# A four-layer network on one core: the low half of each weight slab, subtracted by POOL instead of DVE in the stages that convolve

## The reference

```python
x = x + ssd_mixer(rmsnorm(x));   x = x + conv_ffn(rmsnorm(x))          # 528 tokens
x = x + stick_breaking_attention(...);  x = x + conv_ffn(rmsnorm(x))   # 528
x = x + chunked_rel_attention(rmsnorm(x)); x = x + relu2_mlp(rmsnorm(x))  # 512
x = x + gated_deltanet(rmsnorm(x));        x = x + relu2_mlp(rmsnorm(x))  # 512

def conv_ffn(u):      # depthwise causal convolution, 3 taps, behind the up projection
    g, val = split(causal_dwconv(u @ w_up, conv_w, conv_b)); return (silu(g) * val) @ w_down
# ssd_mixer:      silu(causal_dwconv(u @ w_in[xbc])), 4 taps, then a scan; z is not convolved
# gated_deltanet: silu(causal_conv(h @ w_in[qkv])),   4 taps, then a scan; z is not convolved
```

## Time and profile before

| | |
|---|---|
| median of the runs | 3454.03 us |
| the profiled execution's own time | 3458.24 us |
| its span, first to last instruction | 3456.5 us |
| TensorE (PE) busy | 3210.4 us, 93% of the span |
| VectorE (DVE) busy | 1955.8 us, 57% |
| ScalarE (ACT) busy | 1015.3 us, 29% |
| GpSimd (POOL) busy | 412.0 us, 12% |
| `w_low` subtraction on DVE | 426 instructions, 551.9 us, 1297 ns each |

### The profile page before, as it was taken

The page is one execution under the profiler, slowest core; times in us unless marked ns, Lnnn a source line. Parts: engine busy times, 40 slices in busy tenths (PEclk is TensorE's granted clock), DMA queues, the critical chain, the costliest instruction groups (busy, mean ns, idle before and its releaser), DMA issues.

```text
span 3456.5 us, 49739 instructions
## 1 busy us (share of the span) xinstructions
PE 3210.4 (93%) x19456; PEld 2758.6 (80%) x19456; DVE 1955.8 (57%) x2939; ACT 1015.3 (29%) x1634; POOL 412.0 (12%) x446
## 2 busy tenths in 40 slices
PE   6997879999999999989996999999998988899998
PEld 6995559999998777889995667788876677778886
DVE  5746874647573333574666555544466666664444
ACT  3233332322232434331222333222232522232221
POOL 2000222000020111300005001100010122220002
PEclk9998989999999999999998999999999999999999
DMA  3220002222221000122222222222222200022222
GB/s 115 85 85 31 1 13 91 80 80 85 92 92 62 25 25 31 57 78 90 87 86 73 74 74 68 85 97 91 97 85 79 67 1 1 1 73 97 91 97 79
DMA packets 64344, 235.14 MB, mean 68 GB/s; under 512 B 7248, under 2 KB 7248, under 8 KB 63952
## 3 DMA queue, kind: packets, MB, share of 16 engines
q1 hardware_dynamic: 62928, 229.05, 19.9%
q0 software_dynamic: 1280, 4.20, 0.4%
HBM read 231.12 MB, written 2.10 MB: 67 GB/s over the span
## 4 chain that ended last, share of the span: by engine, by line
PE 58%; DVE 14%; issue 6%; ACT 5%; POOL 2%; DVEq 1%; ACTq 0%; POOLq 0%
PE ps L268 35%; PE ps L297 8%; DVE conv_acc L322 5%; ACT w_high L230 3%; PE ps L1031 2%; PE ps L1024 2%; DVE conv_acc L319 1%; PE ps L1046 1%; PE ps L1014 1%; PE ps L1331 1%; PE ps L1678 1%; PE ps L1359 1%; POOL sqa L377 1%; PE ps L1673 1%; DVE t L436 1%
## 5 line engine op out<-in xcount | busy, mean ns | idle before, releaser
L268 PE MATMUL ps<-x_hi,w_high 128*128 128x264 f32 (+1 forms) x2968 | 764.2, 318 | 71.1 <-DVE w_low L235 33.2
L268 PE MATMUL ps<-x_lo,w_high 128*128 128x264 f32 (+1 forms) x2968 | 755.9, 315 | 0.0
L268 PE MATMUL ps<-x_hi,w_low 128*128 128x264 f32 (+1 forms) x2968 | 754.9, 315 | 0.0
L235 DVE TENSOR_TENSOR w_low<-w_raw,w_high 128x1024 fp32r<-128x1024 f32 x426 | 551.9, 1297 | 262.0 <-ACT w_high L230 261.1
L268 PEld LDWEIGHTS ps<-x_hi,w_high 128*128 128x128 f32 x2968 | 489.8, 189 | 126.9 <-issue 57.7
L230 ACT ACTIVATE w_high<-w_raw 128x1024 fp32r<-128x1024 f32 x426 | 446.0, 1050 | 435.0 <-DMA w_raw<-in_slabs 423.7
L268 PEld LDWEIGHTS ps<-x_lo,w_high 128*128 128x128 f32 x2968 | 487.8, 189 | 34.5 <-issue 1.9
L268 PEld LDWEIGHTS ps<-x_hi,w_low 128*128 128x128 f32 x2968 | 488.8, 190 | 33.3
L268 PE MATMUL ps<-mid_hi,w_high 128*128 128x264 f32 (+1 forms) x1280 | 374.3, 338 | 22.1 <-DVE mid_lo L421 20.5
L268 PE MATMUL ps<-mid_lo,w_high 128*128 128x264 f32 (+1 forms) x1280 | 374.6, 338 | 0.0
L268 PE MATMUL ps<-mid_hi,w_low 128*128 128x264 f32 (+1 forms) x1280 | 373.6, 337 | 0.0
(11 more groups left out here) (339 smaller groups left out, 4323.3 us busy)
## 6 DMA issues: line engine op xcount, KB each, us to landing
w_raw<-in_slabs SPq DMA_DIRECT2D x426, 512.0 KB, 3.3
rel_bias<-in_rel POOLq DMA_DIRECT2D x16, 256.0 KB, 2.9
h<-in_x SPq DMA_DIRECT2D x1, 2112.0 KB, 8.6
out_y<-h SPq DMA_DIRECT2D x8, 256.0 KB, 2.1
consts<-in_consts SPq DMA_DIRECT2D x1, 1032.0 KB, 13.1
par<-in_params SPq DMA_DIRECT2D x1, 346.5 KB, 9.0
```

Of the source, the lines that this page charges most:

```text
L235: dve.tensor_tensor(w_low[:, n % RING, :], w_raw[:, n % RING, :], w_high[:, n % RING, :].bitcast(F32), ALU.subtract).then_inc(S("w_lo"), 1)
L268: mm = pe.matmul(ps[:, 2 * tslot + k, 0:n], w, a[:, kb, c:c + n], start=first, stop=fin)
```

## The change

In the 136 steps of the convolving stages the subtraction leaves DVE's queue and goes into POOL's. `lows_pool` is the same loop of four slabs on POOL: wait for `w_hi`, subtract, count up `w_lo`. Since two engines now count up one counter, the engine that takes over first waits until the other has done its share (`lows_begin`). In `dn_v` POOL's loop is written out, so that five squares of the l2 norm stand between the subtractions. Nothing else changes on ACT, TensorE or SP.

```diff
+        def lows_begin(eng, name):
+            eng.wait_ge(S("w_lo"), SLAB0[name] + AHEAD)
+        def lows_pool(pool, name):
+            lows_begin(pool, name)
+            steps(pool, name, lambda j, i: slab_lo(pool, SLAB0[name] + j, i))
...
                     take_scaled(dve, name, j, i, pad[:, j % 2, 3:3 + LA], LA)
-                    slab_lo(dve, SLAB0[name] + j, i)
                     conv_taps(dve, name, j, i, 3, lambda t: rcol("ffn_conv_w", tile * 3 + t, 12 * i), conv0, LA)
...
                 pair += k
+                lows_begin(dve, f"ffn{layer}_down{r}")
                 residual_dve(dve, f"ffn{layer}_down{r}", LA, split if r == 2 else None)
...
                 take_scaled(dve, name, j, i, pad[:, j % 2, 3:3 + T], T)
-                slab_lo(dve, SLAB0[name] + j, i)
                 dve.wait_ge(S("conv_used"), first + j + 1 + 4 * i)
...
+            lows_begin(dve, "z")
             scaled_stage_dve(dve, "z", lambda k: tile_of(z_t, k, LA), LA)
...
         def ssd_pool(pool):
             stats_pool(pool, 0, LA)
+            lows_pool(pool, "bc")
+            lows_pool(pool, "xs")
...
+            lows_begin(dve, "dn_z")
...
         def dn_pool(pool):
-
+            lows_pool(pool, "dn_qk")
+            lows_begin(pool, "dn_v")
+            for j in range(2):
+                slab_lo(pool, SLAB0["dn_v"] + j)
...
                     .then_inc(S("l2_sq"), 1)
+                if t < 5:
+                    for j in (2 + t,) if t < 4 else (6, 7):
+                        slab_lo(pool, SLAB0["dn_v"] + j)
...
             def pool(e):
+                for r in range(len(FFN_ROUNDS)):
+                    lows_pool(e, f"ffn{layer}_up{r}")
                 stats_pool(e, n_next, LA)
```

## The result

The changed kernel takes 3446.72 us (median of 12 runs, 3433.23 to 3449.17) beside 3459.0 us for the kernel before (12 runs, 3450.45 to 3466.95): ratio 0.9963, 95% interval 0.995 to 0.9975. It is faster by 0.37%, inside the range of 3419 to 3465 but above the forecast's own 3420 to 3443, on the side that was held likeliest, and by about half of what was forecast: 12.3 us between the medians where the sum said 24.

What follows compares the result with a forecast made beforehand. PE is busy 93%; convolving stages lie above its pace, `xs` by a ring through DVE and ACT. Terms -9.6 - 11 - 4 + 0.2 = -24 us took the profiled 3458.2 to 3434, median 3430; range 3419 to 3465.

Steps and rivals of the forecast that it cites:

- the ring through ACT: Convolving stages: DVE's taps wait for ACT's copy, 6.32 us a slab in `xs` against PE's 5.87; the change cuts this.
- POOL and DVE exclude each other: When both read two things in SBUF, each waits for the other's whole instruction, less overlaps of 0.14 and 0.19 us.
- The term D: Length of one POOL subtraction of 1024 columns: taken as 2.3 us, lowest 2.07, highest 2.6; delays DVE by D - 0.47.
- The prediction's own table: Whole kernel's time by length of POOL's subtraction: 2.07 gives about 3421 us, 2.4 gives 3440, 2.5 3453, 2.6 3466.
- `up1`, `up2`: nothing, but without slack: Both feed-forward layers, 56 slabs: four DVE steps take 23.2 us against PE's 23.5, so no gain or loss.
- one of them hides under the wait or a take: `up1`, `up2`: of four subtractions one is hidden by 0.7 to 0.9 us, bringing four DVE steps from 24.0 to 23.2.
- the path from the last tile to `mid_lo`: `down1`, `down2`: exchanges 1.23 and 0.50 us of waiting for 1.83, with DVE behind by part of a step: +1.3 each.
- `dn_qk` 96 us: Deltanet: DVE bounds, 16 steps of 5.75 us plus some 4 us for the start give 96 us, -9.
- `dn_z` and `dn_out` untouched: Deltanet stages without the moved subtraction: forecast to change by 0.
- Rival 2: Slower: feed-forward stages lose their cover from a POOL subtraction of 2.42 us on; at 2.6, +12 us, 3466; chance 0.14.
- rival 3: POOL gets its turn only when DVE is idle; +1 us or more on 136 slabs, beyond 3550 us; chance 0.02.
- rival 4: The change does less than it says, because POOL is held by what stands ahead in its queue; no chance given.

Runs made afterwards that it cites:

- e4_up0: The changed kernel, but in `up1` and `up2` of both feed-forward layers DVE subtracts again; 3433.21 us, ratio 0.9937 to the kernel before.
- e3_ffn: The kernel before, with POOL subtracting in the `up` rounds of the two feed-forward layers alone; 3461.29 us, ratio 1.0015.
- e2_dn: The kernel before, with POOL subtracting in `dn_qk` and `dn_v` alone; 3444.62 us, ratio 0.9972.
- b1_bench: The changed kernel plus nine POOL subtractions of 1024 to 256 columns at its end, engines at rest; 1024 columns took 2337 ns (plain output).
- b2_place: The changed kernel plus four POOL subtractions at its end in the ring's own slots, the first two beside DVE products reading PSUM; 2352, 2354, 2342, 2342 ns.
- e5_same: The changed kernel, but POOL subtracts `w_high` from itself, so the low halves are zero (price probe); 3411.26 us, ratio 0.9866 to the kernel before.

## Why the prediction was right in kind and too high in size

1. *What bounds the kernel, and that the ring through ACT is cut*: right. `xs` -7.2 us (forecast -7.1), `z` -2.0 (forecast -2.1). `bc` was to gain 0.4 and lost 0.4.
2. *POOL and DVE exclude each other, and overlap a little where they hand over*: right. POOL's subtraction at 822.49 ends at 824.90; DVE's first tap behind it ends at 825.19 and needs 0.49, so it began at 824.70, 0.20 before POOL's end (0.19 forecast from the earlier trace rows).
3. *The term D*: 2.3 was taken; it is 2.34 alone and 2.39 to 2.43 in the network. Hence a delay of 1.90 instead of 1.83, and 5.84 instead of 5.75 for DVE's step in the deltanet. The Trainium skill (GPSIMD Engine Reference, "Performance versus the Vector engine") gave 2.4 by its ratio of 1.96; the trace agrees with it (2.39 / 1.22 = 1.96), and the prediction was wrong to set it aside. The prediction's own table gives 3440 for D = 2.4, that is, -14 us. It comes near the measured -12 to -14 partly by chance, since that table still counts what the next point shows to be missing.
4. *"`up1`, `up2`: nothing, but without slack"*: the step that failed. It had four steps of DVE at 23.2 us against PE's 23.5. Measured are 24.28 (24.0 to 24.3 from the second step on, in both layers). 4 x 0.08 = 0.3 of the difference of 1.1 is D. The larger part, about 0.7, is the deduction "one of them hides under the wait or a take (0.7 to 0.9)": the four delays add up to 7.46 where 4 x 1.90 is 7.60, so 0.14 was hidden. A subtraction that begins beside a take still outlasts it by 1.9 us and holds up the first tap. At D = 2.3 the four steps would still be 24.28 - 0.3 = 24.0, above PE's pace, by this working (not run). DVE falls behind by 0.8 us in four slabs, which PE meets in part in `up1` itself and in part in the round that follows: PE waits in the changed kernel's `ffn0_down1` (us in total, times, longest)

```profile
PE ps L276 <- DVE mid_lo L429: 3.5, 1, 3.5
```

   in its first slab, where it waited 2.31 before. The clock is not what was lost: behind the stall the granted clock falls in both kernels, to a mean of 0.83 over 8.5 us here (row below) and of 0.80 over 8.5 us before (856.8 to 865.3), between its half and its full level:

```profile
847.50:856.00 8.50, 8.50 (x61) 8.50 (x61) 3.27 (x5) 1.17 (x2) 0.00 (x0) 0.83 0.18 62
```

   e4_up0 undoes this one step and comes to -22 us, though its own stall there is 2.9 us and so not wholly back at 2.31; e3_ffn shows the step without the mixers. In the same four rounds the prediction's own cost for the path from the last tile to `mid_lo`, +1.3 each, comes out larger too (+7.4 in the table where it had +5.2), which fits a DVE that comes to them later.
5. *`dn_qk` 96 us*: 98.8. Of the 2.8, 16 x 0.09 = 1.4 is D. The other 1.4 is the clock at the start, and belongs to the profiled execution, not to the change: in the same place e2_dn, with the same instructions, has the clock at 1.00 and passes 59 matmuls where the changed kernel passes 52 (first row: changed kernel; second: e2_dn), and its `dn_qk` takes 97.4. b1_bench and b2_place, which are the changed kernel up to its end, have 1.00 and 97.4 as well, and e3_ffn, where DVE subtracts in `dn_qk`, has 0.89.

```profile
2527.00:2543.00 16.00, 13.93 (x52) 10.53 (x52) 11.34 (x11) 5.39 (x6) 2.37 (x1) 0.89 0.18 66
```

```profile
2527.00:2543.00 16.00, 13.93 (x59) 10.66 (x58) 12.25 (x13) 5.41 (x6) 2.40 (x1) 1.00 0.22 74
```

6. *`dn_z` and `dn_out` untouched*: `dn_z` gained 1.5, and no less in any trace with POOL in `dn_v`. `dn_out`, where the scan runs, lost 2.9 in the profiled execution, where it takes 333.0 us against 330.1 before. In b1_bench and b2_place, with the same code, it takes 330.0 and 330.9, so the 2.9 are scatter between executions.
7. *The rivals.* Rival 2's mechanism, the feed-forward layers losing their cover, is real and sets in below the D = 2.42 that the prediction gave it. Its own formula, 16.7 - 0.9 + 4 x (D - 0.47) = 23.5, gives 2.40, and with nothing hidden 2.17 (an estimate; 1.88 in e5_same keeps the cover, 2.34 here loses it). Since the mixers won nearly what was forecast, it took half of the gain and not all. No sign of rival 3 (POOL is never starved: it waits for one DVE instruction at most) or rival 4.

## What to carry to other kernels

When work moves to POOL while DVE works on SBUF, what it costs DVE here is POOL's length less about 0.47 us, once for every instruction; no further part of it is to be written off as hidden unless a row shows both side by side. Move it only into stages where DVE's step plus that delay stays below what bounds the stage, and check this stage by stage: the same edit won 8 and 10 us in two mixers and lost 5 to 7 in the feed-forward layers. And cut POOL's instruction: two halves between DVE's dependent instructions delayed it less than the whole, although POOL itself took longer, and took the gain from 0.4% to 1.0%.

## What the runs showed of the hardware that was not expected

- The same subtraction with one tile as both inputs takes 1.88 us instead of 2.34 (b1_bench); with two inputs a column costs 2.11 ns.
- POOL's 1024 columns take some 0.05 us longer beside a busy PE (2.39 to 2.40 most often) than alone or with PE at rest (2.34); their place, DVE at work on PSUM (0.01, b2_place), ACT and the loads don't explain it.
- DVE's TENSOR_SCALAR, with one input in SBUF, is held up by POOL just as the taps with two inputs are (0.49 becomes 2.06 above). The words of the prediction, "when both read two things", leave it out, though its own have one such tap at 1.27.
- A delay depends on the phase: 1.57 us where POOL begins beside a take, 1.90 between two taps, 2.08 where it begins just before a tap (815.79 and 815.90).
